# GpSimd takes three weight remainders and half of the rotated keys of an attention stage; two sums of squares move to the middle of a norm's features

## The chip, the cores and the metric

The kernel runs as one launch on one core of a Trainium2 chip. The metric is the device time of that launch in microseconds (us). The engines are named as in the profile: PE (TensorE, matrix products, PEld its weight loads), DVE (VectorE), ACT (ScalarE), POOL (GpSimd), SP (SyncE, whose queue issues the weight transfers). SBUF is the memory that all of them read; PSUM is the one that PE writes and that POOL cannot read.

## The reference

Four transformer blocks in a row work on 256 positions of width 1024, all in float32. Cut to the parts that the change touches:

```python
def mla_mixer(hn, pos, w_in, g_q_lat, w_uq, g_kv_lat, w_ukv, g_qn, g_kn, w_o):
    z = hn @ w_in
    c_q, c_kv, k_pe = z[..., :512], z[..., 512:768], z[..., 768:]
    q  = (rms_norm(c_q, g_q_lat) @ w_uq).reshape(b, s, 16, 96)
    kv = (rms_norm(c_kv, g_kv_lat) @ w_ukv).reshape(b, s, 16, 128)
    k = concatenate([kv[..., :64], broadcast(k_pe)], -1)      # 64 plain + 32 rotated parts
    q, k = rms_norm(q, g_qn), rms_norm(k, g_kn)               # per head
    q, k = rope on the last 32 parts of each
    o = block_causal_attention(q, k, kv[..., 64:])            # softmax per head, 16 heads
    return o.reshape(b, s, 1024) @ w_o
```

Around it stand SwiGLU layers (f0 to f3 in the kernel's names), gates with an embedding (p0, p1), a second attention mixer (fox) and a last block (b2), each behind an RMS norm (n0 to n8). b2 begins with norm n8: `x * rsqrt(mean(x*x) + eps)`, times a gain, then a product with a wide matrix.

## The kernel before, in words

**Weights.** All products are made from split numbers. A weight group is 128 x 2048 floats, transferred by SP into `raw`, a ring of four slots. ACT rounds it into `wh` (signal `hi_done`), DVE takes the remainder `wl = raw - wh` (signal `lo_done`), and PE multiplies three times: `wh` by the rounded activations, `wl` by them, and `wh` by their remainders (L614 to L616, L647 to L651, L926 to L934). PE waits for a group by `lo_done` (`wait_group`). SP refills a slot when `lo_done` says its remainder is made; ACT reuses a slot of `wh` when PE has set `w_used`. Each engine runs its own program in the written order, and semaphores are the only links. No scheduler moves anything.

**MLA heads.** The 16 heads run as a software pipeline over four engines. For head j: PE turns queries and keys of the head into PSUM (`turned`, L690), ACT and DVE copy them out (`copy_queries` L1682, `copy_keys` L2305), PE makes the scores (`scores`, L842 to L845), DVE reduces them to negated maxima and scales these by the inverse norm of the queries (`maxima`, L2313, L2314, and L2317 `nmx<-mxp,hrs`), ACT makes the exponentials (`exponentials`, L1692), PE turns them (`probabilities`), DVE copies them out (`copy_turned`, L2324) and takes reciprocals, PE multiplies by the values (`values`, L863), DVE writes the output (`outputs`, L2332). DVE's step i does `maxima(i-1)`, `copy_keys(i)`, `copy_turned(i-2)`, `outputs(i-3)`; PE's step i does `turned(i)`, `scores(i-1)`, `probabilities(i-2)`, `values(i-3)`. The first steps are written out in `begin`, steps from 6 on run in a loop.

The kernel begins this pipeline when only the first eight heads are ready. The second eight heads' sums, inverse norms and scalings are made inside it: DVE sums squares (`sum_keys`, `sum_queries`), POOL makes inverse norms (`inverse_rms`, L2808, L2809, where L2809 is a power) and rotates the queries (L2849 to L2852), DVE scales the keys (`scale_keys`: L2245 for the 64 plain parts, L2246 for the 32 rotated ones). `maxima(8)` waits for POOL's last inverse norm. In steps 8 to 18, DVE also makes the remainders of the weight groups g+11, g+12 and g+13 (three quarters of `mla_w_o`), a quarter of a group in a step (`split_quarter`, L1994). PE first needs group g+11 in `o_high(2)`, after the last head.

**Norm n8.** PE turns x into PSUM in pieces of 128 positions by 128 features. ACT rounds each piece, times its gain, into `zh` (`round_x`, L1505), and DVE takes the remainder `zl` (`rest_x`, L2030). `BY_FEATURES` is the order of the 16 pieces: feature block k, and within it t = 0, 1. After the 16th piece ACT makes two sums of squares (`squares`, L1493), then rounds the next weight groups of b2, which PE waits for.

Of the kernel before, what the change touches and what calls it, by code (L numbers as in the profile page):

```python
# [18 lines left out]
F32 = mybir.dt.float32  # L19
# [3 lines left out]
ALU = mybir.AluOpType  # L23
# [3 lines left out]
P = 128  # L27
S = 256
NT = S // P
# [5 lines left out]
H = 16  # L35
QR, KVR, ROPE, NOPE = 512, 256, 32, 64
DQ = NOPE + ROPE
# [5 lines left out]
RING = 4  # L43
GC = 2048
# [62 lines left out]
PLAN, NGROUPS = plan()  # L107
# [43 lines left out]
def build(nc, I, out):  # L151
    with ExitStack() as ctx:
        def sem(name):
            return ctx.enter_context(nc.semaphore(name))
# [11 lines left out]
        raw = sb("raw", [P, RING, GC])  # L166
        wh = sb("wh", [P, RING, GC], F32R)
        wl = sb("wl", [P, RING, GC], F32R)
        h = sb("h", [P, NT, D])
# [22 lines left out]
        hrs = sb("hrs", [P, 4, H])  # L192
# [30 lines left out]
        kn = x("kn", [P, NT, H * DQ])  # L223
# [10 lines left out]
        kpe = x("kpe", [P, NT, ROPE])  # L234
# [97 lines left out]
        hi_done = sem("hi_done")  # L332
        lo_done = sem("lo_done")
# [26 lines left out]
        heads_ss = sem("heads_ss")  # L360
        heads_rstd = sem("heads_rstd")
        heads_ready = sem("heads_ready")
        q_rotated = sem("q_rotated")
        max_done = sem("max_done")
        exp_done = sem("exp_done")
# [210 lines left out]
        BY_FEATURES = [(t, k) for k in range(DK) for t in range(NT)]  # L576
# [12 lines left out]
        def _(pe):  # L589
# [359 lines left out]
            g, q, f, r = PLAN["mla"]  # L949
# [53 lines left out]
            def mla_ready(i):  # L1003
                if i % 8 == 0:
                    pe.wait_ge(q_rotated, i // 8 + 1)
                    pe.wait_ge(heads_ready, NT * (i // 8 + 1))
                    fill = q + MLA_KV_FILL[i // 8] + 1
                    pe.wait_ge(acc_read[fill % 2], acc_reads(fill))

# [66 lines left out]
            g, q, f, r = PLAN["fox"]  # L1076
# [73 lines left out]
            s = (g + 2) % RING  # L1150
            for k in range(DK):
                w = slice(k * H, (k + 1) * H)
# [6 lines left out]
            for n in range(1, 6):  # L1159
                fill = q + fox_fill(n)  # L1160
                open_acc(fill)
                for k in range(2):
                    w = fox_group(n) + k
# [65 lines left out]
            g, q, f, r = PLAN["b2"]  # L1229
# [97 lines left out]
            for c in range(len(B2_CHUNKS)):  # L1327
# [6 lines left out]
                for k in range(2):  # L1334
                    w = 2 * c + k
# [103 lines left out]
        def _(act):  # L1439
# [3 lines left out]
            done = [2]  # L1443
# [47 lines left out]
            def squares(r, t):  # L1491
                rows_ready(act, r, t)
                act.activation(hn[:, t, :], h[:, t, :], ACT.Square, accum_out=ssq[:, t:t + 1])\  # L1493
                   .then_inc(sq_done, 1)
# [94 lines left out]
            g, q, f, r = PLAN["mla"]  # L1589
# [151 lines left out]
            def ple(name, nname, r, after, r_after):  # L1741

                g, q, _, _ = PLAN[name]

                def sigmoids(t):
                    for n in range(2):
                        tile_ready(act, q + n, t, g + 3)
                        act.activation(gate[:, t, 512 * n:512 * n + 512], acc(q + n, t), ACT.Sigmoid,
                                       scale=scaled(r, t)).then_inc(acc_read[(q + n) % 2], 1)

                norm(nname, r, lambda t: split_to(g + 4), True)
                for t in range(NT):
                    squares(r, t)
                sigmoids(0)
                split_to(g + 7)
                sigmoids(1)
                if after != "n8":
                    norm(after, r_after)
                    return

                for t, k in BY_FEATURES:
                    round_x(after, r_after, t, k)
                for t in range(NT):
                    squares(r_after, t)

            ple("p0", "n3", 3, "n4", 4)
            ffn("f2", 4)
# [3 lines left out]
            g, q, f, r = PLAN["fox"]  # L1771
# [38 lines left out]
            for n, c in enumerate(FOX_CHUNKS):  # L1810
                w, fill = fox_group(n), q + fox_fill(n)
# [40 lines left out]
            g, q, f, r = PLAN["b2"]  # L1852
# [112 lines left out]
        def _(dve):  # L1965
# [16 lines left out]
            def split(g, i=0):  # L1982
# [2 lines left out]
                dve.wait_ge(hi_done, g - 1 + RING * i)  # L1985
                dve.tensor_tensor(wl[:, s, 0:n], raw[:, s, 0:n], wh[:, s, 0:n].bitcast(F32), ALU.subtract)\  # L1986
                   .then_inc(lo_done, 1)

            def split_quarter(n):

                g = done[0]
                s, w = g % RING, slice(n * GC // 4, (n + 1) * GC // 4)
                dve.wait_ge(hi_done, g - 1)
                e = dve.tensor_tensor(wl[:, s, w], raw[:, s, w], wh[:, s, w].bitcast(F32), ALU.subtract)  # L1994
                if n == 3:
                    e.then_inc(lo_done, 1)
                    done[0] += 1

            def split_half(n):

# [239 lines left out]
            def scale_keys(c, t):  # L2240

                dve.wait_ge(heads_rstd, 2 * NT * c + t + 1)
                kv = heads3(kn[:, t, :], DQ)[:, 8 * c:8 * c + 8]
                by = hrs[:, 2 + t, 8 * c:8 * c + 8].unsqueeze(2)
                dve.tensor_tensor(kv[:, :, 0:NOPE], kv[:, :, 0:NOPE], by.to_broadcast([P, 8, NOPE]), ALU.mult)  # L2245
                dve.tensor_tensor(kv[:, :, NOPE:DQ], kpe[:, t, :].unsqueeze(1).to_broadcast([P, 8, ROPE]),  # L2246
                                  by.to_broadcast([P, 8, ROPE]), ALU.mult).then_inc(heads_ready, 1)


            def keys_values(c, n):  # L2250
# [124 lines left out]
            def rest_rows(done, banks):  # L2375

                for b in banks:
                    t = b // 2
                    dve.wait_ge(oh_done, done + b + 1)
                    dve.tensor_tensor(xl[:, b % 2::2, t * P:(t + 1) * P],  # L2380
                                      M[:, b, :].rearrange("p (k n) -> p k n", k=4),
                                      xh[:, b % 2::2, t * P:(t + 1) * P].bitcast(F32), ALU.subtract)\
                       .then_inc(m_read[b], 1)

            def matrix_out(g, q, r, nname):

                residual(q, g + 3, 1.0, 0)
                split_to(g + 6)
                rest(nname, r, 0)
                residual(q, g + 3, 1.0, 1)  # L2390
                split_to(done[0] + 1)
                rest(nname, r, 1)
# [3 lines left out]
            for i in range(6, H + 3):  # L2396
                if i == H + 2:
                    rest_rows(OH["mla"], range(1))
                step(i)

                if i == 6:
                    scale_keys(1, 1)
                elif i == 7:
                    sum_queries(1, 1)
                elif i >= 8:
                    split_quarter((i - 8) % 4)
                if i == H + 2:
                    split_quarter(3)
            rest_rows(OH["mla"], range(1, 4))
            matrix_out(g + 10, q + 10 + H, 2, "n2")  # L2410
            ffn("f1", 2, "n3")

# [384 lines left out]
        def _(pool):  # L2797
            steps = [0]

            def link(ins):  # L2800

                steps[0] += 1
                ins.then_inc(p_step, 1)
                pool.wait_ge(p_step, steps[0])

            def inverse_rms(dst, src, n, width, signal):

                link(pool.tensor_scalar(dst, src, 1.0 / width, EPS, ALU.mult, ALU.add))  # L2808
                pool.tensor_tensor(dst, dst, mhalf[:, 0:n], ALU.pow).then_inc(signal, 1)  # L2809
# [25 lines left out]
            for c in range(2):  # L2835
                for t in range(NT):
                    pool.wait_ge(heads_ss, 2 * NT * c + t + 1)
                    inverse_rms(hrs[:, 2 + t, 8 * c:8 * c + 8], hss[:, 2 + t, 8 * c:8 * c + 8], 8, DQ, heads_rstd)
                for t in range(NT):
                    for n in (2 * c, 2 * c + 1):  # L2840
                        fill = PLAN["mla"][1] + MLA_Q_FILL[n]
                        pool.wait_ge(acc_read[fill % 2], acc_reads(fill))
                    qv = qn[:, t, :].rearrange("p (h d) -> p h d", d=DQ)[:, 8 * c:8 * c + 8]
                    tb = [tab[:, 0, t, j, :].unsqueeze(1).to_broadcast([P, 8, 16]) for j in range(4)]
                    x1, x2 = qv[:, :, NOPE:NOPE + 16], qv[:, :, NOPE + 16:DQ]
                    pool.wait_ge(heads_sq, 2 * NT * c + NT + t + 1)
                    m4 = [rt[:, 2 * t + m // 2, 8 * (m % 2):8 * (m % 2) + 8, :] for m in range(4)]
                    for m, (x, j) in enumerate(((x1, 0), (x2, 1), (x1, 2), (x2, 3))):
                        e = pool.tensor_tensor(m4[m], x, tb[j], ALU.mult)  # L2849
                    link(e)  # L2850
                    pool.tensor_tensor(x1, m4[0], m4[1], ALU.subtract)
                    e = pool.tensor_tensor(x2, m4[2], m4[3], ALU.add)  # L2852
                    if t:
                        e.then_inc(q_rotated, 1)
                    else:
                        link(e)
                for t in range(NT):
                    pool.wait_ge(heads_ss, 2 * NT * c + NT + t + 1)
                    inverse_rms(hrs[:, t, 8 * c:8 * c + 8], hss[:, t, 8 * c:8 * c + 8], 8, DQ, heads_rstd)
            pool.wait_ge(m_ready[3], PLAN["n2"][2][3])  # L2860
            pool.wait_ge(table_out, 16)
            pool.dma_start(p_n[:, :, :], I["p"][0, 0].rearrange("(t p) n -> p t n", p=P)).then_inc(p_in, 16)
# [153 lines left out]
```

## Time and profile before

| | us |
|---|---|
| median of 3 runs | 1336.75 (1336.58 to 1338.41) |
| the profiled execution | 1337.19 |
| its span | 1335.4 |
| PE busy | 1316.5, 99% of the span |
| PEld busy | 1078.3, 81% |
| DVE busy | 798.0, 60% |
| ACT busy | 679.4, 51% |
| POOL busy | 128.8, 10% |

PE is on the chain that ended last for 88% of the span, DVE for 5%, ACT for 3%. The granted TensorE clock has a mean of 0.998 of full speed. The profiled execution lies 0.44 us above the median, and 1.8 us of it lie outside the span. The matmuls' ends overlap, so PE's pace is read from the distance of starts, not from durations. In the rows below a time at the start is us from the span's start, and what stands in brackets is the idle time of the engine just before and what ended it.

### The profile page before, as it was taken

What the parts mean: (1) busy time and instruction counts of PE and PEld (TensorE: products, weight loads), DVE (VectorE), ACT (ScalarE), POOL (GpSimd) and SP (SyncE); (2) the same over time, 40 slices, a digit from 0 to 9 for tenths busy, and PEclk for the clock granted to TensorE, in tenths of its full rate; (3) what the DMA queues carried; (4) which work ended last, traced back from release to release, by engine and by line L of the source; (5) the groups of instructions that cost most, each with busy time, mean ns of one, the idle gap of its engine ahead of it and who ended that gap; (6) DMA issues with size and microseconds to landing.
All of it is one profiled execution on the core that took longest, in us unless ns stands there. A gap on an engine that the chain in (4) does not pass through costs nothing.

```text
span 1335.4 us, 17481 instructions
## 1 busy us (share of the span) xinstructions
PE 1316.5 (99%) x6474; PEld 1078.3 (81%) x6474; DVE 798.0 (60%) x1036; ACT 679.4 (51%) x959; POOL 128.8 (10%) x199
## 2 busy tenths in 40 slices
PE   8999999999999999999999999999999999999997
PEld 6888788788888887888888777888888877788886
DVE  6755448885555546655544667655554655665674
ACT  6444427755444426644444557544443646457542
POOL 2000002712000000000000330100000042110000
PEclk9999999999999999999999999999999999999999
DMA  9665544336655654555553654466564397555441
GB/s 299 219 188 189 189 154 165 98 95 190 204 182 184 218 194 144 180 186 187 180 204 126 227 183 127 134 188 188 188 220 160 128 266 246 167 163 172 160 158 32
DMA packets 148782, 236.46 MB, mean 177 GB/s; under 512 B 10087, under 2 KB 103447, under 8 KB 148208
## 3 DMA queue, kind: packets, MB, share of 16 engines
q1 hardware_dynamic: 143600, 222.26, 51.1%
q0 software_dynamic: 4736, 12.96, 3.3%
q8 instruction: 40, 0.66, 0.2%
q10 hardware_dynamic: 384, 0.41, 0.1%
q14 instruction: 22, 0.18, 0.0%
HBM read 233.43 MB, written 4.51 MB: 178 GB/s over the span
## 4 chain that ended last, share of the span: by engine, by line
PE 88%; DVE 5%; ACT 3%; issue 2%; DMA 1%; POOL 0%; SPq 0%; POOLq 0%; DVEq 0%; ACTq 0%
PE acc L614 19%; PE acc L616 19%; PE acc L615 19%; PE acc L647 7%; PE acc L648 7%; PE acc L651 7%; PE misc L690 5%; DVE wl L1986 2%; ACT wh L1461 1%; PE misc L1270 1%; DMA raw<-in_ffn_w_in_dram 1%; PE misc L1127 1%; ACT xh L1505 0%; DVE pT L2324 0%; ACT hn L1493 0%
## 5 line engine op out<-in xcount | busy, mean ns | idle before, releaser
L1986 DVE TENSOR_TENSOR wl<-raw,wh 128x2048 fp32r<-128x2048 f32 (+2 forms) x201 | 453.2, 2261 | 266.0 <-ACT wh L1461 265.9
L1461 ACT ACTIVATE wh<-raw 128x2048 fp32r<-128x2048 f32 (+2 forms) x207 | 388.7, 1888 | 138.8 <-PE acc L651 124.7
L614 PE MATMUL acc<-wh,xh 128*128 128x512 f32 (+1 forms) x832 | 329.0, 395 | 2.8 <-DVE xl L2030 1.3
L616 PE MATMUL acc<-wh,xl 128*128 128x512 f32 (+1 forms) x832 | 323.2, 388 | 0.0
L615 PE MATMUL acc<-wl,xh 128*128 128x512 f32 (+1 forms) x832 | 322.6, 388 | 0.0
L614 PEld LDWEIGHTS acc<-wh,xh 128*128 128x128 f32 x832 | 156.3, 188 | 36.9 <-DVE wl L1979 4.4
L616 PEld LDWEIGHTS acc<-wh,xl 128*128 128x128 f32 x832 | 156.2, 188 | 32.8
L615 PEld LDWEIGHTS acc<-wl,xh 128*128 128x128 f32 x832 | 156.5, 188 | 30.1
L647 PE MATMUL acc<-wh,ah 128*128 128x512 f32 x320 | 125.7, 393 | 0.0
L648 PE MATMUL acc<-wl,ah 128*128 128x512 f32 x320 | 124.6, 389 | 0.0
L614 PE MATMUL acc<-wh,zh 128*128 128x512 f32 x272 | 108.5, 399 | 1.5 <-DVE wl L1986 1.0
L616 PE MATMUL acc<-wh,zl 128*128 128x512 f32 x272 | 106.2, 390 | 0.0
L615 PE MATMUL acc<-wl,zh 128*128 128x512 f32 x272 | 106.0, 390 | 0.0
L1550 ACT ACTIVATE ah<-misc 128x512 f32 (+1 forms) x44 | 26.4, 599 | 156.0 <-PE misc L690 156.0
L651 PE MATMUL acc<-wh,al 128*128 128x512 f32 x320 | 98.5, 389 | 0.0
L2808 POOL TENSOR_SCALAR rstd<-ssq 128x1 f32<-128x1 f32 x19 | 9.4, 493 | 924.4 <-ACT hn L1493 924.4
L1544 ACT ACTIVATE sg<-acc,rstd 128x256 f32<-128x256 f32 x88 | 41.4, 475 | 100.5 <-PE acc L616 100.5
L2146 DVE TENSOR_TENSOR al<-misc,ah 128x512 f32 (+1 forms) x44 | 30.4, 692 | 84.0 <-ACT ah L1550 84.0
L1505 ACT ACTIVATE xh<-misc,gains 128x128 fp32r<-128x128 f32 x128 | 40.4, 364 | 68.8 <-PE misc L690 59.7
L647 PEld LDWEIGHTS acc<-wh,ah 128*128 128x128 f32 x320 | 60.1, 188 | 13.8 <-issue 1.7
L651 PEld LDWEIGHTS acc<-wh,al 128*128 128x128 f32 x320 | 60.1, 188 | 12.6
L648 PEld LDWEIGHTS acc<-wl,ah 128*128 128x128 f32 x320 | 60.1, 188 | 12.2
(363 smaller groups left out, 1654.1 us busy)
## 6 DMA issues: line engine op xcount, KB each, us to landing
raw<-in_ffn_w_in_dram SPq DMA_DIRECT2D x172, 512.0 KB, 4.7
raw<-in_ffn_w_out_dram SPq DMA_DIRECT2D x88, 512.0 KB, 4.4
raw<-in_w_in_dram SPq DMA_DIRECT2D x64, 512.0 KB, 4.8
raw<-in_fox_w_in_dram SPq DMA_DIRECT2D x24, 512.0 KB, 4.4
raw<-in_ple_w_gate_dram SPq DMA_DIRECT2D x16, 512.0 KB, 4.1
raw<-in_mla_w_o_dram SPq DMA_DIRECT2D x8, 512.0 KB, 4.1
raw<-in_fox_w_o_dram SPq DMA_DIRECT2D x8, 512.0 KB, 4.5
raw<-in_w_out_dram SPq DMA_DIRECT2D x8, 512.0 KB, 4.4
```

The lines of the kernel that those rows point to most:

```text
L614: pe.matmul(dst, hi, rhs_h, start=first, stop=False)
L615: pe.matmul(dst, hi, rhs_l, start=False, stop=False)
L616: return pe.matmul(dst, lo, rhs_h, start=False, stop=last)
L647: pe.matmul(acc(q + n, t), xa, wh[:, s, r], start=st, stop=False)
L648: pe.matmul(acc(q + n, t), xa, wl[:, s, r], start=False, stop=False)
L651: mm = pe.matmul(acc(q + n, t), xb, wh[:, s, r], start=False, stop=en)
L690: return pe.transpose(M[0:rows, b, cols], src, m[:, :])
L1461: act.activation(wh[:, s, 0:n], raw[:, s, 0:n], ACT.Copy).then_inc(hi_done, 1)
L1505: act.activation(x_cols(xh, r, k, t), turned(r, k, t), ACT.Copy, scale=gains[:, c:c + 1]).then_inc(xh_done, 1)
L1544: act.activation(sg[:, c % 2, t, :], acc(q, t)[:, 0:256], ACT.Silu, scale=rstd[:, t:t + 1]).then_inc(silu_done, 1)
L1986: dve.tensor_tensor(wl[:, s, 0:n], raw[:, s, 0:n], wh[:, s, 0:n].bitcast(F32), ALU.subtract)\
L2146: dve.tensor_tensor(al[:, bass.ds(i * 4 + 2 * c, 2), :], pair(M[:, b, :]), ah[:, bass.ds(i * 4 + 2 * c, 2), :].bitcast(F32), ALU.subtract)\
```

## The change

It has three parts. (1) The remainders of weight groups g+11 to g+13 are no longer made by DVE in quarters; POOL makes them whole, one instruction of 128 x 2048 each, behind its last inverse norm of the heads. DVE waits for all three before it goes on to the output product. (2) For the second eight heads, the rotated part of the scaled keys is made by POOL, between the rotated queries and the queries' inverse norms. PE waits for it before it turns head 8. (3) In norm n8 the two sums of squares stand behind the 9th and the 10th piece instead of behind the 16th.

```diff
@@ mla_ready (PE)
                     pe.wait_ge(heads_ready, NT * (i // 8 + 1))
+                    if i:
+                        pe.wait_ge(keys_rotated, NT)
@@ ple, norm n8 (ACT)
-                for t, k in BY_FEATURES:
+                for n, (t, k) in enumerate(BY_FEATURES):
                     round_x(after, r_after, t, k)
-                for t in range(NT):
-                    squares(r_after, t)
+                    if n in (8, 9):
+                        squares(r_after, n - 8)
@@ scale_keys (DVE): the rotated part only for the first eight heads
+                if c == 0:
+                    e = dve.tensor_tensor(kv[:, :, NOPE:DQ], kpe[...], by[...], ALU.mult)
+                e.then_inc(heads_ready, 1)
@@ DVE, loop over the heads' steps
-                elif i >= 8:
-                    split_quarter((i - 8) % 4)
-                if i == H + 2:
-                    split_quarter(3)
             rest_rows(OH["mla"], range(1, 4))
+            dve.wait_ge(lo_done, g + 12)
+            done[0] = g + 14
@@ POOL, behind the rotated queries
+                if c:
+                    pool.wait_ge(heads_ready, NT)
+                    pool.wait_ge(heads_rstd, 2 * NT * c + NT)
+                    for t in range(NT):
+                        ...
+                        pool.tensor_tensor(kv[:, :, NOPE:DQ], kpe[...], by[...], ALU.mult)\
+                            .then_inc(keys_rotated, 1)
                 for t in range(NT):
                     pool.wait_ge(heads_ss, 2 * NT * c + NT + t + 1)
                     inverse_rms(...)
@@ POOL, behind the heads
+            g = PLAN["mla"][0]
+            for n in range(g + 11, g + 14):
+                pool.wait_ge(hi_done, n - 1)
+                pool.wait_ge(lo_done, n - 2)
+                pool.tensor_tensor(wl[:, n % RING, :], raw[:, n % RING, :], wh[:, n % RING, :].bitcast(F32),
+                                   ALU.subtract).then_inc(lo_done, 1)
```

DVE, one step of the heads' loop and the start of the next, before (L1994 is the quarter of a remainder, L2317 the scaled maxima):

```order
L2313 TENSOR_REDUCE mxp<-acc 128x1
L2314 TENSOR_REDUCE mxp<-acc 128x1
L2317 TENSOR_TENSOR nmx<-mxp,hrs 128x2
L2305 TENSOR_SCALAR qkT<-misc,headg 96x256
L2324 COPY pT<-misc 128x384
L2326 RECIPROCAL rin<-rs 128x2
L2332 TENSOR_TENSOR hn<-misc,rin 128x2x64
L1994 TENSOR_TENSOR wl<-raw,wh 128x512
L2313 TENSOR_REDUCE mxp<-acc 128x1
```

The same place now, where the scaled maxima are L2314:

```order
L2310 TENSOR_REDUCE mxp<-acc 128x1
L2311 TENSOR_REDUCE mxp<-acc 128x1
L2314 TENSOR_TENSOR nmx<-mxp,hrs 128x2
L2302 TENSOR_SCALAR qkT<-misc,headg 96x256
L2321 COPY pT<-misc 128x384
L2323 RECIPROCAL rin<-rs 128x2
L2329 TENSOR_TENSOR hn<-misc,rin 128x2x64
L2310 TENSOR_REDUCE mxp<-acc 128x1
```

The quarter behind `outputs` is gone from the step, and the rest keeps its order.

POOL, from the second eight heads' last rotated queries to the transfers behind the heads, before:

```order
L2849 TENSOR_TENSOR rt<-qn,tab 128x128 x4
L2851 TENSOR_TENSOR qn<-rt 128x8x16
L2852 TENSOR_TENSOR qn<-rt 128x8x16
L2808 TENSOR_SCALAR hrs<-hss 128x8
L2809 TENSOR_TENSOR hrs<-hrs,mhalf 128x8
L2808 TENSOR_SCALAR hrs<-hss 128x8
L2809 TENSOR_TENSOR hrs<-hrs,mhalf 128x8
L2862 DMA p_n<-in_p_dram 128x2x256
```

The same place of POOL now, with the keys (L2860) and the remainders (L2870):

```order
L2845 TENSOR_TENSOR rt<-qn,tab 128x128 x4
L2847 TENSOR_TENSOR qn<-rt 128x8x16
L2848 TENSOR_TENSOR qn<-rt 128x8x16
L2860 TENSOR_TENSOR kn<-kpe,hrs 128x8x32 x2
L2804 TENSOR_SCALAR hrs<-hss 128x8
L2805 TENSOR_TENSOR hrs<-hrs,mhalf 128x8
L2804 TENSOR_SCALAR hrs<-hss 128x8
L2805 TENSOR_TENSOR hrs<-hrs,mhalf 128x8
L2870 TENSOR_TENSOR wl<-raw,wh 128x2048 x3
L2874 DMA p_n<-in_p_dram 128x2x256
```

The two key instructions stand ahead of both inverse norms of the queries, the three long remainders behind them.

ACT at norm n8, now (before, the 16 `zh` stand in one row of x16 with both sums of squares behind it):

```order
L1751 ACTIVATE gate<-acc,rstd 128x512 x2
L1508 ACTIVATE zh<-misc,gains 128x4x32 x9
L1496 ACTIVATE hn,ssq<-h 128x1024
L1508 ACTIVATE zh<-misc,gains 128x4x32
L1496 ACTIVATE hn,ssq<-h 128x1024
L1508 ACTIVATE zh<-misc,gains 128x4x32 x6
L1464 ACTIVATE wh<-raw 128x2048 x4
```

Both sums of squares now stand ahead of the last six pieces, and the weight groups follow the 16th piece directly.

## Rows read from the trace of the kernel before

**Rows 1.** Busy time in a stretch: PE, PEld, DVE, ACT, POOL, clock, DMA.

```profile
272.00:280.00 8.00, 7.85 (x64) 6.63 (x62) 7.81 (x27) 6.01 (x18) 0.00 (x0) 1.00 0.00 1
```

**Rows 2.** Chain that ended last, in the heads' loop: start, us, what.

```profile
276.52 0.60 DVE wl L1994
277.32 0.34 DVE mxp L2314
```

**Rows 3.** Timeline of DVE in the heads: scaled maxima of heads 8, 10, 11, 15; a quarter.

```profile
272.58 0.16 DVE L2317 TENSOR_TENSOR nmx<-mxp,hrs 128x2 f32<-128x2 f32 x1
...
277.69 0.16 DVE L2317 TENSOR_TENSOR nmx<-mxp,hrs 128x2 f32<-128x2 f32 x1
...
278.92 0.68 DVE L1994 TENSOR_TENSOR wl<-raw,wh 128x512 fp32r<-128x512 f32 x1
...
280.17 0.16 DVE L2317 TENSOR_TENSOR nmx<-mxp,hrs 128x2 f32<-128x2 f32 x1
...
290.09 0.17 DVE L2317 TENSOR_TENSOR nmx<-mxp,hrs 128x2 f32<-128x2 f32 x1
```

**Rows 4.** Timeline of PE in the heads' loop: scores, turned heads, scores again.

```profile
255.28 0.39 PE L842 MATMUL acc<-qkT 96*128 96x128 f32 x2
...
275.85 0.49 PE L842 MATMUL acc<-qkT 96*128 96x128 f32 x2
...
277.73 0.38 PE L690 MATMUL misc<-ident,qn 128*96 128x128 f32 x2
277.95 0.38 PE L690 MATMUL misc<-ident,kn 128*96 128x128 f32 x2
278.33 0.49 PE L842 MATMUL acc<-qkT 96*128 96x128 f32 x2
```

**Rows 5.** Timeline of DVE, the second eight heads' rotated keys.

```profile
263.30 0.67 DVE L2246 TENSOR_TENSOR kn<-kpe,hrs 128x256 f32<-128x256 f32 x1
...
266.38 0.41 DVE L2246 TENSOR_TENSOR kn<-kpe,hrs 128x256 f32<-128x256 f32 x1
```

**Rows 6.** Timeline of POOL in and ahead of the heads.

```profile
230.59 0.20 POOL L2808 TENSOR_SCALAR hrs<-hss 128x8 f32<-128x8 f32 x1 [8.22 <-DVE hss L2232]
...
246.28 3.56 POOL L2809 TENSOR_TENSOR hrs<-hrs,mhalf 128x8 f32<-128x8 f32 x1
...
252.21 1.64 POOL L2809 TENSOR_TENSOR hrs<-hrs,mhalf 128x8 f32<-128x8 f32 x1
...
260.58 0.46 POOL L2849 TENSOR_TENSOR rt<-qn,tab 128x128 f32<-128x128 f32 x1
...
261.00 0.88 POOL L2849 TENSOR_TENSOR rt<-qn,tab 128x128 f32<-128x128 f32 x2
...
269.90 1.65 POOL L2809 TENSOR_TENSOR hrs<-hrs,mhalf 128x8 f32<-128x8 f32 x1
```

**Rows 7.** Timeline of DVE, instructions that lie beside those of POOL.

```profile
246.04 2.29 DVE L1986 TENSOR_TENSOR wl<-raw,wh 128x2048 fp32r<-128x2048 f32 x1
...
253.58 0.16 DVE L2317 TENSOR_TENSOR nmx<-mxp,hrs 128x2 f32<-128x2 f32 x1
...
260.68 0.38 DVE L2317 TENSOR_TENSOR nmx<-mxp,hrs 128x2 f32<-128x2 f32 x1
```

**Rows 8.** Chain that ended last, behind norm n8.

```profile
1069.42 2.18 ACT hn L1493 x4
1071.60 1.82 ACT wh L1461
1073.44 2.30 DVE wl L1986
```

**Rows 9.** Timeline of PE and of ACT around norm n8.

```profile
1075.88 0.47 PE L614 MATMUL acc<-wh,zh 128*128 128x512 f32 x1 [0.96 <-DVE wl L1986]
...
1067.32 0.62 ACT L1505 ACTIVATE zh<-misc,gains 128x128 fp32r<-128x128 f32 x2 [1.23 <-DVE zl L2030]
```

**Rows 10.** Busy time and granted clock (third last number) behind PE's last product.

```profile
1328.00:1330.00 2.00, 0.00 (x0) 0.00 (x0) 0.42 (x1) 0.72 (x2) 0.56 (x2) 0.91 0.00 0
```

More of the change, by code:

```diff
@@ L362, in build @@
         heads_ready = sem("heads_ready")
+        keys_rotated = sem("keys_rotated")
         q_rotated = sem("q_rotated")
@@ L1987, in split @@
                    .then_inc(lo_done, 1)
[L1989 to L1997, printed above, removed]
             def split_half(n):
@@ L2244, in scale_keys @@
                 by = hrs[:, 2 + t, 8 * c:8 * c + 8].unsqueeze(2)
-                dve.tensor_tensor(kv[:, :, 0:NOPE], kv[:, :, 0:NOPE], by.to_broadcast([P, 8, NOPE]), ALU.mult)
-                dve.tensor_tensor(kv[:, :, NOPE:DQ], kpe[:, t, :].unsqueeze(1).to_broadcast([P, 8, ROPE]),
-                                  by.to_broadcast([P, 8, ROPE]), ALU.mult).then_inc(heads_ready, 1)
+                e = dve.tensor_tensor(kv[:, :, 0:NOPE], kv[:, :, 0:NOPE], by.to_broadcast([P, 8, NOPE]), ALU.mult)
+                if c == 0:
+                    e = dve.tensor_tensor(kv[:, :, NOPE:DQ], kpe[:, t, :].unsqueeze(1).to_broadcast([P, 8, ROPE]),
+                                          by.to_broadcast([P, 8, ROPE]), ALU.mult)
+                e.then_inc(heads_ready, 1)
             def keys_values(c, n):
@@ L2856, in _ @@
                         link(e)
+                if c:
+                    pool.wait_ge(heads_ready, NT)
+                    pool.wait_ge(heads_rstd, 2 * NT * c + NT)
+                    for t in range(NT):
+                        kv = kn[:, t, :].rearrange("p (h d) -> p h d", d=DQ)[:, 8 * c:8 * c + 8]
+                        by = hrs[:, 2 + t, 8 * c:8 * c + 8].unsqueeze(2)
+                        pool.tensor_tensor(kv[:, :, NOPE:DQ], kpe[:, t, :].unsqueeze(1).to_broadcast([P, 8, ROPE]),
+                                           by.to_broadcast([P, 8, ROPE]), ALU.mult).then_inc(keys_rotated, 1)
                 for t in range(NT):
```

## The prediction

> **What bounds the kernel now.** I first read the busy times: PE is busy for 99% of the span, so only time in which PE waits, or a stage whose pace another engine sets, can be gained. The list of waits by engine then shows where PE waits at all. Two places matter here.
>
> The first is the heads' loop. In [rows 1] PE and DVE both look full, 7.85 and 7.81 of 8 us, so busy shares do not tell which one leads. The chain does: in the loop it runs through DVE's quarter of a remainder and DVE's maxima [rows 2]. One head takes 280.17 - 277.69 = 2.48 us on DVE [rows 3], and DVE never rests. PE has a small gap: its scores start at 275.85, its last pair of turned tiles at 277.95, and such a pair takes 0.22 (277.73 to 277.95), so PE could go on at 278.17 but does at 278.33 [rows 4]. PE's own work is 2.32 us a head. Where PE did not have to wait, the first two score products are 0.10 shorter (0.39 against 0.49) [rows 4], so its floor is 2.22 to 2.32; I take 2.27.
>
> The second is the beginning of the last block. PE stands still for 0.96 us there for a weight remainder [rows 9]. The chain behind it is ACT's sums of squares, 2.18 us, then ACT's rounding, then DVE's remainder [rows 8].
>
> **Part 1, the three remainders.** Removed from DVE: twelve quarters, 0.60 us of the path each (0.68 with its overlap) [rows 2, 3], eight of them between the maxima of heads 7 and 15. DVE's step falls from 2.48 to 1.88, below PE's 2.27, so PE becomes the bound of a free-running loop. The gain there is 2.48 - 2.27 = 0.21 a head.
>
> Added on POOL: three subtractions of 128 x 2048. No row has one. POOL's nearest is the product of 128 x 128 in two SBUF inputs, whose starts lie 0.42 apart (260.58, 261.00) [rows 6]. The fixed part of a POOL instruction is at most the 0.20 of its shortest scaling [rows 6], which leaves 0.22 for 128 elements, and 0.20 + 16 x 0.22 = 3.7 us for 2048. With no fixed part it is 16 x 0.42 = 6.7 us. A fixed part of 0.15 gives 4.5 us; I take this, near the low end, because some of the 0.20 is the scaling's own work but a fixed part there must be. Three of them are 13.5 us. POOL is free for them: its last inverse norm ends at 269.90 + 1.65 = 271.55 [rows 6], and PE wants the first of the three groups only after head 15's maxima at 290.09 [rows 3]. By time alone POOL's work is hidden, with some 5 us to spare, and the slots of `raw` come free no later than now. The wait that DVE gets behind the heads is then met long before. The Trainium skill has 4497 ns for this very size (GPSIMD Engine Reference, "Elementwise — side-by-side cycle accounting"); no run here shows it yet, and by it the sum would be the same.
>
> What is not hidden is the memory path that POOL and DVE share. Two rows show it. POOL's power of 128 x 8 takes 1.64 us alone, but 3.56 when it is issued 0.24 after DVE has begun a subtraction with two SBUF inputs that runs from 246.04 to 248.33 [rows 6, 7]: POOL stood for the whole rest of DVE's instruction. The other way round, DVE's `nmx`, with two SBUF inputs of two elements each, is 0.16 long everywhere in the loop, but 0.38 at 260.68, where it ends at 261.06, just when POOL's product of 260.58 gives way to the next at 261.00 [rows 6, 7]. Two elements need no bandwidth; DVE waited until that POOL instruction was through, and was let in before the following one. So I read: a DVE instruction with two SBUF inputs waits for the end of a POOL instruction that is reading SBUF. Against it stands one row: `nmx` at 253.58 is not delayed inside POOL's power of 252.21 to 253.85 [rows 6, 7]. That power reads only 8 elements and computes for the rest, so its reading was over; a subtraction of 2048 elements reads to its end.
>
> The Trainium skill states it as a rule that speaks against this change (SBUF — State Buffer, "Who interferes with whom"): a DVE instruction with two SBUF inputs and a GpSimd instruction that reads SBUF exclude each other for a whole instruction, whichever came first. By that rule, the rows for 128 elements agree; for 2048 no run here shows it.
>
> In DVE's step `nmx` is that instruction, and everything is queued behind it: ACT's exponentials of the head wait for it, and `copy_keys` of the next head, for which PE's next scores wait. Now the sum. The queries' last inverse norm ends about 271.3 (0.3 earlier, part 2). The first subtraction begins there; `nmx` of head 8, before at 272.58, wants to run at about 272 and waits until 271.3 + 4.5 = 275.8. Once it is through (about 0.15 for the handover), the second subtraction begins. `nmx` of head 9 comes 2.3 us later (keys, scores, maxima), inside it, and waits until 280.4. Head 10 waits likewise until 285.1, and ends at about 285.3. Before it ended at 277.85 [rows 3]: 7.4 later. From head 10 to 15 five heads run at 2.27 instead of 2.48, which gives back 1.05. Part 1 with its price: +6.4 us. With subtractions of 3.7 it is +4.0, with 5.3 +8.8, with 6.7 +13.
>
> **Part 2, the rotated keys.** DVE loses 0.67 + 0.41 busy [rows 5], of which 0.60 and 0.33 lie on its path. POOL gets two products of 128 x 256, by the same rate 0.7 us each (0.64 to 0.84), behind the rotated queries. The first of them lies just where `nmx` of head 5 now comes and holds it back by about 0.6, so I count 0.3 gained, not 0.9. POOL is done with them more than 1 us before PE turns head 8, so the new wait costs nothing; were it not so, PE would lose a few tenths. POOL's first inverse norm of the queries comes 1.4 later and has 4 us of rest behind it to absorb that. The 0.3 is in the start of 271.3 above and otherwise vanishes in the stall of head 8. Bounds for the part alone: 0 to 0.9 gained.
>
> **Part 3, the squares.** ACT rests 1.23 us before 1067.32 and about as long before the piece ahead of it [rows 9]; both rests were for DVE or PE. One sum of squares is 2.18 / 2 = 1.09 us of the path. Both fit in the rests, and the last six pieces come about 0.1 later. PE has several products in hand for each piece and does not wait in this stretch, so a tenth is hidden. ACT's rounding for the group that PE waits for begins about 2 us sooner, so the 0.96 of PE's waiting [rows 9] goes. What is late next is nothing: PE follows with the small products for the row norms, whose inverse norms also come sooner. Gain 0.9, bounds 0 (if a transfer sets the group) and 0.96. POOL's transfers behind n8 start 2 to 3 us sooner and meet the weight loads; PE has several us in hand there.
>
> **Sum.** +6.4 - 0.9 = +5.5 on the profiled execution's 1337.19: 1342.7; on the median 1336.75: 1342.2 us. Its own range, from subtractions of 3.7 to 5.3 us and part 3 between 0 and 0.96, is 1339.8 to 1345.6.
>
> **The rivals.**
>
> *Rival 1, `nmx` slips through (faster).* If POOL's reads leave room for a two-element read, no head is held. Then `nmx` of head 8 runs at 272.0 instead of 272.58, seven heads to head 15 run at 2.27 instead of 17.51 / 7 = 2.50 [rows 3], together -2.2; with part 3, -3.1: 1333.7 us. For it: `nmx` at 253.58. Against it: the 0.22 at 260.68 for two elements, and POOL's 1.9 us of standing at 246.28.
>
> *Rival 2, the stall also costs clock or is longer (slower still).* PE rests 2 to 3.4 us at a time in the three stalls. At the end of the kernel PE has no work from 1328.00 on, and the granted clock has a mean of 0.91 over 1328 to 1330 [rows 10]: it falls from full (2.4 GHz) to half (1.2 GHz) at about 1329.6. If that happens in the heads, some PE steps behind the stalls run at half speed: 2 to 4 us more, 1345 to 1346. If POOL starts its next subtraction before DVE is let in, head 8 waits for all three: 271.3 + 13.5 = 284.8 instead of 272.6, less the gains: +12.2 - 1.5 - 0.9, 1346.6. Against it: DVE was let in at 261.00.
>
> *Rival 3, the lock is held in pieces (no change).* If DVE waits about 1 us each time, three or six such waits eat the gains: about 1336.5 us. Only a POOL instruction that pauses in its reading would do so; no row shows one.
>
> **How the numbers follow.** A difference of 0.2%, 2.7 us, is about what a measurement of this kernel can tell from none. Forecast 0.68, rival 1 0.20, rival 2 0.07, rival 3 0.05. Faster by over 0.2%: rival 1 with most of its weight (its 3.1 us are just over the bound) and nothing else, 0.17. Within: the rest of rival 1, rival 3, a small part of the forecast, 0.12. Slower: 0.71. The time is the forecast's, 1342.2. The range has to take in rival 1 to leave out no more than 2 in 10: 1333.3 to 1346.5.
>
> **What would show it.** In the profile of the changed kernel: `nmx` instructions of 2 to 4 us for heads 8, 9 and 10, each ending with a POOL subtraction of about 4.5 us; PE's scores 4.6 us apart there and 2.3 apart from head 11 on; the last `nmx` at about 296.5 instead of 290.09; no PE wait of 0.96 at the third group of the last block. If `nmx` stays at 0.16 beside a subtraction, my reading of the shared path is wrong and rival 1 holds. If the subtractions are far from 4.5 us, the size is wrong threefold.

## The result and the profile after

| | us | against before |
|---|---|---|
| before, median of 4 runs | 1336.74 | |
| after, median of 4 runs (1342.9 to 1346.11) | 1343.8 | 1.0052 [1.004, 1.0065] |
| the profiled execution of after | 1342.9 | before 1337.19 |
| its span | 1341.1 | before 1335.4 |

The change makes the kernel slower by 7.1 us; 1342.2 was predicted. The two profiled executions differ by 5.7 us: the profiled execution of after is the fastest of its four.

First the stretch of [rows 1] in the changed kernel: length, then PE, PEld, DVE, ACT, POOL busy, granted clock, DMA share, GB/s.

```profile
272.00:280.00 8.00, 3.41 (x20) 2.81 (x20) 7.51 (x10) 2.94 (x9) 7.71 (x3) 0.79 0.41 131
```

PE worked 7.85 of these 8 us before, in 64 instructions, and 3.41 now, in 20. DVE's 7.51 are in 10 instructions instead of 27: it is "busy" because it stands inside one of them. The timeline of DVE shows which; these are the scaled maxima of heads 5, 8, 9, 10, 11, 12, 13 and 15, and answer to [rows 3]:

```profile
263.27 0.34 DVE L2314 TENSOR_TENSOR nmx<-mxp,hrs 128x2 f32<-128x2 f32 x1
...
271.24 3.51 DVE L2314 TENSOR_TENSOR nmx<-mxp,hrs 128x2 f32<-128x2 f32 x1
...
276.98 2.43 DVE L2314 TENSOR_TENSOR nmx<-mxp,hrs 128x2 f32<-128x2 f32 x1
...
282.53 1.55 DVE L2314 TENSOR_TENSOR nmx<-mxp,hrs 128x2 f32<-128x2 f32 x1
...
287.18 0.16 DVE L2314 TENSOR_TENSOR nmx<-mxp,hrs 128x2 f32<-128x2 f32 x1
...
289.67 0.17 DVE L2314 TENSOR_TENSOR nmx<-mxp,hrs 128x2 f32<-128x2 f32 x1
...
292.10 0.16 DVE L2314 TENSOR_TENSOR nmx<-mxp,hrs 128x2 f32<-128x2 f32 x1
...
296.96 0.16 DVE L2314 TENSOR_TENSOR nmx<-mxp,hrs 128x2 f32<-128x2 f32 x1
```

The timeline of POOL for the same time (the keys' rotated part, its last inverse norm, the remainders):

```profile
262.99 1.18 POOL L2860 TENSOR_TENSOR kn<-kpe,hrs 128x256 f32<-128x256 f32 x2
...
268.62 1.64 POOL L2805 TENSOR_TENSOR hrs<-hrs,mhalf 128x8 f32<-128x8 f32 x1
270.22 13.83 POOL L2870 TENSOR_TENSOR wl<-raw,wh 128x2048 fp32r<-128x2048 f32 x3
```

The wide view gives the three subtractions in one row; narrower windows give the second and third apart:

```profile
274.88 4.52 POOL L2870 TENSOR_TENSOR wl<-raw,wh 128x2048 fp32r<-128x2048 f32 x1
...
279.54 4.51 POOL L2870 TENSOR_TENSOR wl<-raw,wh 128x2048 fp32r<-128x2048 f32 x1
```

Add the durations. The maxima of heads 8, 9 and 10 end at 271.24 + 3.51 = 274.75, 276.98 + 2.43 = 279.41 and 282.53 + 1.55 = 284.08. The subtractions end at 270.22 + 4.51 = 274.73, 279.40 and 284.05. Three instructions that need 0.16 us each end within 0.03 us of a GpSimd instruction's end, and DVE is let in before GpSimd's next one begins (274.88, 279.54).

PE stands behind them. Its scores in the timeline, to be read against [rows 4]:

```profile
275.20 0.49 PE L843 MATMUL acc<-qkT 96*128 96x128 f32 x2 [3.26 <-DVE qkT L2302]
...
284.52 0.80 PE L843 MATMUL acc<-qkT 96*128 96x128 f32 x2
...
287.99 0.39 PE L843 MATMUL acc<-qkT 96*128 96x128 f32 x2
...
290.32 0.49 PE L843 MATMUL acc<-qkT 96*128 96x128 f32 x2
...
292.75 0.49 PE L843 MATMUL acc<-qkT 96*128 96x128 f32 x2
```

The wait is put down to `qkT`, DVE's copy of the keys, which stands behind `nmx` in DVE's order. The same two products take 0.80 at 284.52 and 0.49 later: the clock had fallen. Two-microsecond windows of the same columns show when:

```profile
276.00:278.00 2.00, 2.00 (x15) 1.91 (x13) 1.64 (x3) 1.19 (x2) 2.00 (x1) 0.67 0.88 254
...
284.00:286.00 2.00, 1.98 (x8) 1.30 (x7) 1.19 (x5) 1.45 (x5) 0.05 (x1) 0.50 0.35 80
286.00:288.00 2.00, 2.00 (x16) 1.82 (x15) 1.44 (x5) 0.62 (x3) 0.00 (x0) 0.77 1.05 351
288.00:290.00 2.00, 2.00 (x20) 1.84 (x19) 1.45 (x7) 0.96 (x4) 0.00 (x0) 1.00 0.36 128
```

A mean of 0.67 over 276 to 278 puts the fall from full to half level (2.4 to 1.2 GHz) at 276.7, after PE had done nothing from 271.9 to 275.2. The 0.77 puts the return at 286.9.

In the last block, the place of [rows 9] has no wait any more: PE goes from its small products for the norm to the next group's.

```profile
1080.49 1.08 PE L1352 MATMUL misc<-ident,rstd 128*1 128x64 f32 x8
1081.50 0.50 PE L615 MATMUL acc<-wh,zh 128*128 128x512 f32 x1
```

**Where the time went.** I take the distance from `nmx` of head 4 (start 260.68 before, 260.01 after) to `nmx` of head 15 (290.09 [rows 3], 296.96): 29.41 before, 36.95 after, +7.54 us. The last block gives back 0.96. The changed run also reached the heads 0.67 earlier. Of this, 0.64 is there already in the kernel's first 28 us (PE starts the same product at 27.72 before and at 27.08 after), far ahead of anything that was changed; in the ten experiments that product starts anywhere between 26.99 and 27.67. So this part is chance. 7.54 - 0.96 - 0.67 = 5.9, against 5.7 of difference in span.

### The profile page after: what moved, and what is told of

It reads as the page before. It is cut to its first block, busy times and chain, and to the rows that moved or that the text cites. A ratio compares the mean times of both kernels' runs of the same rounds, so it can differ in the third digit from the quotient of the medians.

```text
span 1341.1 us, 17477 instructions
## 1 busy us (share of the span) xinstructions
PE 1320.5 (98%) x6474; PEld 1082.0 (81%) x6474; DVE 797.5 (59%) x1022; ACT 679.1 (51%) x959; POOL 145.0 (11%) x204
## 3 DMA queue, kind: packets, MB, share of 16 engines
HBM read 233.43 MB, written 4.51 MB: 177 GB/s over the span
## 4 chain that ended last, share of the span: by engine, by line
PE 90%; DVE 4%; ACT 3%; issue 2%; DMA 0%; POOL 0%; SPq 0%; POOLq 0%; DVEq 0%; ACTq 0%
PE acc L615 20%; PE acc L617 19%; PE acc L616 19%; PE acc L648 7%; PE acc L649 7%; PE acc L652 7%; PE misc L691 5%; DVE wl L1990 1%; ACT wh L1464 1%; PE misc L1273 1%; PE misc L1130 1%; PE acc L845 1%; DMA raw<-in_ffn_w_in_dram 0%; ACT xh L1508 0%; PE misc L864 0%
```

## The experiments

**The theories.** Their letters are those of the expectations below. A is the forecast's: a DVE instruction with two SBUF inputs waits for the whole of a GpSimd instruction that reads SBUF, and all of the loss is behind that. Its rivals: B, the loss comes from something else in the change (the keys on POOL, the squares). C, every DVE instruction that reads SBUF waits for a GpSimd subtraction. And one without a letter: the loss comes from bandwidth or transfers, in which case it would depend neither on the form of `nmx` nor on the length of POOL's instructions. What was open besides is why the pace behind the stalls was not what I had forecast. Theory D is about that: scores, maxima, keys and the next scores follow one another, and this ring sets the pace once DVE has no quarters to make. All ratios below are against the kernel before, run on the same chip beside the experiment; a ratio is known to about 0.1%, some 1.2 us.

**1. Part 1 undone.** The rest of the change (keys on POOL, squares moved) stays.

```diff
+                elif i >= 8:
+                    split_quarter((i - 8) % 4)
+                if i == H + 2:
+                    split_quarter(3)
...
-            dve.wait_ge(lo_done, g + 12)
-            done[0] = g + 14
...
-                pool.tensor_tensor(wl[:, n % RING, :], raw[:, n % RING, :], wh[:, n % RING, :].bitcast(F32),
-                                   ALU.subtract).then_inc(lo_done, 1)
```

> The changed kernel with part 1 undone: the twelve quarters are back on VectorE, the rotated keys stay on GpSimd, the squares stay in the middle. Theory A (GpSimd's long subtractions hold VectorE's nmx): no nmx over 0.5 us from head 8 on, clock at full in the heads, heads as before less 0 to 0.9 us, last block 0.9 us shorter: 1335.4 to 1336.0 us. Theory B (the rotated keys or the moved squares are what costs): 1340 us or more.

Measured: 1335.65 us, 0.9991 [0.9982, 1.0]. `nmx` is 0.16 to 0.17 from head 8 to 15. The heads are 2.48 apart but for two (2.63 from head 8 to 9, 2.85 from head 10 to 11). The whole loss is part 1, which excludes B.

**2. Part 1 alone on the kernel before.**

```diff
-                elif i >= 8:
-                    split_quarter((i - 8) % 4)
-                if i == H + 2:
-                    split_quarter(3)
...
+            dve.wait_ge(lo_done, g + 12)
+            done[0] = g + 14
...
+                pool.tensor_tensor(wl[:, n % RING, :], raw[:, n % RING, :], wh[:, n % RING, :].bitcast(F32),
+                                   ALU.subtract).then_inc(lo_done, 1)
```

> The kernel before with part 1 alone. Theory A: three nmx of 2.4 to 3.5 us, each ending with a subtraction of 4.6 us, clock at half level behind the second stall, 7.0 to 8.0 us over the kernel before: 1344 to 1345 us. Theory B (the keys on GpSimd or the squares cost): about 1336 us.

Measured: 1346.06 us, 1.0069 [1.0056, 1.0083], 9.3 us over before, where I had expected 7.0 to 8.0. `nmx` of heads 8 to 10 takes 3.51, 2.23 and 1.55, nearly as in after. What differs is the clock, here in windows from 286 and from 290:

```profile
286.00:288.00 2.00, 2.00 (x10) 1.63 (x9) 0.65 (x3) 0.41 (x2) 0.00 (x0) 0.50 0.87 232
...
290.00:292.00 2.00, 2.00 (x17) 1.79 (x17) 0.84 (x4) 0.49 (x2) 0.00 (x0) 0.89 0.00 0
```

It stays at half until about 290.4, 3.5 us longer than in after:

```profile
288.02 0.16 DVE L2317 TENSOR_TENSOR nmx<-mxp,hrs 128x2 f32<-128x2 f32 x1
...
291.79 0.16 DVE L2317 TENSOR_TENSOR nmx<-mxp,hrs 128x2 f32<-128x2 f32 x1
```

From head 11 to 12 it takes 3.77 instead of 2.49 in after: 1.3 us that the same three stalls cost more.

**3. Part 3 alone on the kernel before.**

```diff
+                for n, (t, k) in enumerate(BY_FEATURES):
                     round_x(after, r_after, t, k)
-                for t in range(NT):
-                    squares(r_after, t)
+
+                    if n in (8, 9):
+                        squares(r_after, n - 8)
```

> The kernel before with part 3 alone. Theory A: the PE wait of 0.96 us at the third weight group of the last block is gone and nothing replaces it: 0.9 to 1.0 us under the kernel before, 1335.8 us. Rival: the gain is given back by a later wait for a transfer, 1336.7 us.

Measured: 1335.79 us, 0.9991 [0.9982, 1.0]. The heads are as before (29.40 from head 4 to 15) and PE's longest wait for a remainder at L614 falls from 0.96 to 0.3. That is 1.0 us for part 3, and it leaves 0.14 for part 2, the difference of the medians to experiment 1, which is too small to tell from nothing.

**4. Another form of `nmx`.** One edit on after: two instructions that take the factor as a scalar for each partition, so that none has two SBUF tensors as inputs.

```diff
-                    dve.tensor_tensor(nmx[:, :, j], mx, hrs[:, 0:NT, j], ALU.mult).then_inc(max_done, 1)
+                    for t in range(NT):
+                        e = dve.tensor_scalar(nmx[:, t, j:j + 1], mx[:, t:t + 1], hrs[:, t, j:j + 1], None, ALU.mult)
+                    e.then_inc(max_done, 1)
```

> The changed kernel, but nmx made by two instructions with one SBUF tensor and a pointer scalar each, so that no VectorE instruction in the loop has two SBUF tensors. Theory A (only the second SBUF tensor input collides with GpSimd's reads): no stall, the three subtractions run beside the heads, clock stays full; the added instruction costs 0.1 us a head; about 1336 us, 7 to 8 under the changed kernel. Theory C (any VectorE instruction that reads SBUF waits for a GpSimd subtraction): the stalls of 2.4 to 3.5 us stay, 1343 to 1345 us.

Measured: 1336.05 us, 0.9992 [0.9983, 1.0001]. DVE's maxima of heads 9 to 11, and POOL beside them:

```profile
274.55 0.33 DVE L2315 TENSOR_SCALAR nmx<-mxp,hrs 128x1 f32<-128x1 f32 x2
...
277.11 0.33 DVE L2315 TENSOR_SCALAR nmx<-mxp,hrs 128x1 f32<-128x1 f32 x2
...
279.67 0.33 DVE L2315 TENSOR_SCALAR nmx<-mxp,hrs 128x1 f32<-128x1 f32 x2
```

```profile
270.73 13.88 POOL L2872 TENSOR_TENSOR wl<-raw,wh 128x2048 fp32r<-128x2048 f32 x3
```

The subtractions, the slots and the transfers are those of after, and every stall is gone. This excludes bandwidth and transfers. It excludes C too, since the new instructions read SBUF as well. But the heads are 2.56 apart although DVE has no quarter to make: freeing DVE did not speed up the loop. Some of the 2.56 is the new form, which takes 0.33 for the two instructions instead of 0.16.

**5. The same work in short instructions.** After with each remainder in eight pieces of 256, `nmx` as it was.

```diff
+                for c in range(0, GC, 256):
+                    e = pool.tensor_tensor(wl[:, n % RING, c:c + 256], raw[:, n % RING, c:c + 256],
+                                           wh[:, n % RING, c:c + 256].bitcast(F32), ALU.subtract)
+                e.then_inc(lo_done, 1)
```

> The changed kernel with each GpSimd remainder cut into eight instructions of 128 x 256; nmx is the one with two SBUF tensors again. Theory A (the wait lasts to the end of the GpSimd instruction that is running, and VectorE gets in before the next): each piece takes 0.7 us, 24 of them 16.5 us, nmx is 0.2 to 0.85 long beside them and never more, clock stays full, 1336 to 1338 us. Rival (VectorE waits until GpSimd's whole row of instructions is through): one nmx of 15 us, 1349 us.

Measured: 1336.31 us, 0.9995 [0.9986, 1.0004]. DVE, then POOL:

```profile
273.85 0.51 DVE L2314 TENSOR_TENSOR nmx<-mxp,hrs 128x2 f32<-128x2 f32 x1
...
276.59 0.69 DVE L2314 TENSOR_TENSOR nmx<-mxp,hrs 128x2 f32<-128x2 f32 x1
...
287.90 0.17 DVE L2314 TENSOR_TENSOR nmx<-mxp,hrs 128x2 f32<-128x2 f32 x1
```

```profile
270.18 16.84 POOL L2871 TENSOR_TENSOR wl<-raw,wh 128x256 fp32r<-128x256 f32 x24
```

Now `nmx` waits at most 0.69 - 0.16 = 0.53 us, which is less than one piece (16.84 / 24 = 0.70), and not at all once the pieces are through at 287.02. Same engine, same bytes: what counts is the length of the instruction that holds the path. With experiment 4 this shows A.

**6, 7, 8. DVE copies the keys ahead of the maxima.** If `nmx` only hurt because the keys' copy stands behind it, and if the loop is slow because scores, maxima, keys and the next scores lie in a row, the other order in DVE's step should help. Tried on experiments 4, 5 and 3:

```diff
                 def step(i):
-                    if 0 <= i - 1 < H:
-                        maxima(i - 1)
                     if i < H:
                         copy_keys(i)
+                    if 0 <= i - 1 < H:
+                        maxima(i - 1)
```

> The kernel with the pointer-scaled nmx (e4), and in VectorE's step the keys of head i are copied ahead of the maxima of head i-1. Theory D (without VectorE's quarters one head takes 2.56 us because scores, maxima, keys and the next scores follow one another in series): the pace falls to PE's own 2.2 to 2.35 us a head, nine heads gain 1.9 to 2.5 us, about 1334.0 us. Rival (another bound of VectorE, ScalarE or PE): the pace stays at 2.45 to 2.56, 1336 us.

> The pieces of 128 x 256 (e5) with the keys copied ahead of the maxima. Theory D with A: nmx still waits up to 0.85 us now and then, but off the series that sets the pace, so 2.2 to 2.4 us a head and 1334 to 1335 us. Rival: the waits still show, 1336 us or more.

> The kernel before with the squares moved (e3) and the keys copied ahead of the maxima, the quarters still on VectorE. Theory D: VectorE's own 2.48 us a head is the bound there, so the new order gains nothing to speak of: 1335.8 us, within 0.4 of e3. Rival (the order alone is what counts, wherever the remainders are made): 1334 us.

Measured: 1343.7 us, 1.0051 [1.0038, 1.0065]; 1343.06, 1.0044 [1.0031, 1.0058]; 1341.95, 1.0035 [1.0023, 1.0047]. All three missed by 6 to 10 us. The chain that ended last in experiment 6 tells why:

```profile
267.06 0.37 ACT qkT L1685
...
267.55 0.48 DVE qkT L2302
268.03 0.20 DVE mxp L2310
268.23 0.34 DVE mxp L2311
...
268.72 0.21 DVE nmx L2315
...
269.32 0.74 ACT probs L1695 x3
270.06 0.94 ACT wh L1472
271.00 0.37 ACT qkT L1685
...
271.50 0.48 DVE qkT L2302
```

The keys' copy waits until ACT has copied the queries of the same head, and those stand in ACT's order behind the exponentials of the head two before, which wait for its `nmx`. Put behind the keys, `nmx` closes a longer ring over two engines: 3.95 us a head while ACT also makes halves of weight groups, about 3.0 after. I had looked at DVE's order alone and overlooked ACT's. The clock has a share in two of the three: by its means in windows of two us it is at half level from 275.2 to 285.4 in experiment 6 and from 273.8 to 280.6 in experiment 7, but at full level throughout the heads in experiment 8. So the 6.2 us of experiment 8 over experiment 3 are the order alone; how much of the rest in the other two is the clock is not worked out. A version that drops the keys' wait for the queries was not tried.

**9, 10. The keys of heads 10 to 15 on ACT.** This takes the 0.48 of the keys' copy off the ring scores, maxima, keys, scores, without any change in what waits for what on DVE. Experiment 9 has it on experiment 4, experiment 10 on experiment 1 (part 1 undone).

```diff
+                    if 10 <= i < H:
+                        tb = i % 2
+                        act.activation(qkT[0:DQ, tb, S:2 * S], M[0:DQ, tb, S:2 * S], ACT.Copy,
+                                       scale=headg[0:DQ, 1:2]).then_inc(m_read[tb], 1)
...
-                    if i < H:
+                    if i < 10:
                         copy_keys(i)
```

> The kernel with the pointer-scaled nmx and GpSimd's remainders (e4), and from head 10 on ScalarE copies the keys as well as the queries, so that VectorE's maxima no longer stand between a head's scores and the next head's keys. Theory D (the pace of 2.56 us a head is a series of scores, maxima, keys, scores; the order tried in e6 failed because the keys waited for ScalarE's queries behind the exponentials): with the keys behind the queries on ScalarE the pace falls to PE's own 2.2 to 2.35 us from head 10 on, 1.3 to 2.0 us under e4, 1334.0 to 1334.8 us. Rival (ScalarE's exponentials and two copies become the series): 2.5 us a head or more, 1336 us.

> The same on the kernel with VectorE's quarters (e1): VectorE's step falls from 2.48 to 2.08 us, below PE's. Theory D: 2.2 to 2.35 us a head from head 10 on, 0.8 to 1.6 us under e1, 1334.1 to 1334.9 us, so the remainders need not leave VectorE at all. Rival (as above): 1335.7 us or more.

Measured: 1334.06 us, 0.9976 [0.9966, 0.9986], as expected, and 1333.38 us, 0.997 [0.9959, 0.9982], 0.7 below what I expected. Both are faster than before and after. PE's scores of heads 10 to 12 in experiment 10:

```profile
274.53 0.40 PE L843 MATMUL acc<-qkT 96*128 96x128 f32 x2
...
276.86 0.39 PE L843 MATMUL acc<-qkT 96*128 96x128 f32 x2
...
279.07 0.39 PE L843 MATMUL acc<-qkT 96*128 96x128 f32 x2
```

They are 2.33 and 2.21 apart, and PE runs on: this is the floor of 2.22 to 2.32 that the forecast took from [rows 4]. DVE makes its quarters in this kernel and reaches the floor all the same; with the quarters gone (experiment 9) it is no faster. For theory D the clean comparison is experiment 9 with 4, where DVE was not full in either: 2.56 a head became 2.31 to 2.33. In experiment 10 the keys' copy also leaves a DVE that was full, so that a lighter DVE could have brought the gain there.

The distance from `nmx` of head 4 to head 15, less 1.0 us for part 3, accounts for every kernel within 0.6 us:

| | heads 4 to 15 | difference to before, with part 3 | measured (medians) |
|---|---|---|---|
| before | 29.41 | | |
| after | 36.95 | +6.5 | +7.1 |
| experiment 1 | 29.15 | -1.3 | -1.2 |
| 2 (no part 3) | 38.84 | +9.4 | +9.3 |
| 4 | 29.21 | -1.2 | -0.8 |
| 5 | 30.34 | -0.1 | -0.4 |
| 6 | 36.81 | +6.4 | +7.0 |
| 7 | 36.75 | +6.3 | +6.3 |
| 8 | 35.58 | +5.2 | +5.2 |
| 9 | 27.38 | -3.0 | -2.7 |
| 10 | 27.14 | -3.3 | -3.4 |

## Why the prediction was right, and what in it was wrong

**The mechanism of part 1 was right.** It was read from 0.22 us in one row, `nmx` at 260.68 [rows 7], and 1.9 us in another, POOL's power at 246.28 [rows 6], and experiments 4 and 5 show it. The Trainium skill's rule (SBUF — State Buffer, "Who interferes with whom") is borne out for an instruction of 2048 elements, with 3.51, 2.43 and 1.55 us. It is not borne out for POOL's power. The row that stood against the forecast, `nmx` of 0.16 us inside the power of 252.21 [rows 6, 7], comes again in the changed kernel: `nmx` of head 7 starts at 268.81 and takes 0.17, inside the power of 268.62 to 270.26. That a power is done reading early, as the forecast has it, no run tests.

**The size of a subtraction was right:** 4.5 predicted, 4.51 measured. In part this was a choice: the rows of before bound it only between 3.7 and 6.7, and the fixed part of 0.15 us that makes it 4.5 stands in none of them. With 3.7 or 5.3 the forecast would have been 2.4 us off its own number. The Trainium skill's 4497 ns (GPSIMD Engine Reference, "Elementwise — side-by-side cycle accounting") agrees within 0.02 us.

**Place of the stalls: right within 1.2 us.** I put the first subtraction at 271.3 and the end of `nmx` of head 10 at 285.3; they are 270.22 and 284.08. DVE's steps ahead of head 8 came sooner, 0.67 by chance and as much again by part 2. From `nmx` of head 4 (start) to the end of that of head 10 it is 17.17 us before (260.68 to 277.85) and 24.07 after: +6.9, where the sum had +7.4.

**The failed step is the term behind the stalls.** The prediction says "From head 10 to 15 five heads run at 2.27 instead of 2.48, which gives back 1.05." It counted DVE's and PE's busy time of a step and left out the ring of waits between them, and it put the clock at nothing. From the end of `nmx` of head 10 to the start of that of head 15 it was 12.24 before and is 12.88 after: 0.64 lost, not 1.05 gained. Two things are in it.
- The pace. Free of the quarter, the heads are 2.43 apart (289.67, 292.10), which gives back 0.25. I had compared DVE's busy 1.88 with PE's 2.27 and taken the larger. The loop is neither: DVE waits for PE's scores in each step.

```profile
289.78 0.48 DVE L2302 TENSOR_SCALAR qkT<-misc,headg 96x256 f32<-96x256 f32 x1
...
291.45 0.29 DVE L2310 TENSOR_REDUCE mxp<-acc 128x1 f32<-128x128 f32 x1 [0.46 <-PE acc L846]
```

  Scores, maxima, `nmx`, keys and the next scores follow one another: the keys' copy ends at 290.26, PE's scores run from 290.32 to 291.41, the maxima from 291.45, `nmx` at 292.10, and PE's next scores start at 292.75, 2.43 after the last. The quarter had filled a hole in this ring. Its removal brings 0.05 a head; in experiment 4 the longer `nmx`, which lies in the ring, makes it 2.56. Experiment 9 shows that taking the keys' copy out of the ring brings 0.24 a head.
- The clock, which I had made a rival with 0.07. From the end of `nmx` of head 10 to the start of the next it is 3.10 us (284.08 to 287.18); at full clock it is 2.27 (289.83 to 292.10), and so it was behind the first stall, before the clock fell: 2.23 (274.75 to 276.98), against 3.12 behind the second (279.41 to 282.53). With 2.49 instead of 2.43 for the next head (287.18 to 289.67) that is 0.9 lost. -0.25 + 0.9 = +0.65, the measured 0.64.

**Part 2: right in the total.** The two products with the keys take 1.18 together, below the 0.64 to 0.84 each of the forecast, and `nmx` of head 5 is held for 0.34 - 0.16 = 0.18, not for 0.6. So the heads from 4 to 8 take 11.26 in experiment 1 and 11.89 in experiment 3: 0.63 gained by head 8, not 0.3. But 0.37 of it is gone again at head 11, the 2.85 of experiment 1, for a reason that is open, and 0.25 is left at head 15. The new wait of PE costs nothing.

**Part 3: right.** 0.9 predicted, 0.96 in the trace and 1.0 in experiment 3.

**The sum.** Parts 1 and 2 came to +7.5 in place of +6.4, part 3 to -1.0 in place of -0.9. That the profiled execution (1342.9) lies only 0.2 from the 1342.7 predicted for it is luck: the time behind the stalls was 1.69 above the forecast's, but the stalls came 0.5 under the sum and the start 0.67 early by chance. The median of 1343.8 is 1.6 above the forecast, inside its own range of 1339.8 to 1345.6. The three executions of after without a trace took 0.5 to 3.2 us longer, at a mean granted clock of 0.993 against 0.995 in the profiled one. The 0.9 us of clock are therefore the price in the fastest execution; what it was in the others is not shown.

**The rivals.** Rival 1 (`nmx` slips through) fell with the first stall. Its time of 1333.7 would not have come even so: experiment 4 has no stall and takes 1336.05, since a loop free of quarters does not run at 2.27. (Its longer `nmx` is in that time: at 2.43 a head instead of 2.56 it would be 0.9 less by my estimate, still 1.4 above 1333.7.) Rival 2's half about the clock happened, with 0.9 us where I had 2 to 4; in experiment 2 it was 0.9 + 1.3 = 2.2. PE stood still for 3.26 and 1.40 us in the first two stalls and not at all in the third, where its own work at half clock filled the time. The half about POOL did not happen: its next subtraction always began after DVE's `nmx`. Rival 3 did not happen in the change, but experiment 5 is that case made on purpose; it came to 1336.31, where I had given 1336.5.

**What stays open:** why the half clock lasted 3.5 us longer in experiment 2 than in after, with stalls of nearly the same length and place; and what held head 11 back by 0.37 us in experiment 1.

## What to carry to other kernels

Idle time of GpSimd was not free here, because its instructions shared something with one on the path. Before moving work to GpSimd, look at every DVE instruction with two SBUF inputs that will run beside it, however small, at what is queued behind it, and at the length of each single GpSimd instruction. If the work must go there, give the small DVE instruction its factor as a per-partition scalar, or cut GpSimd's work into short pieces; the first took every stall away here, the second left at most 0.53 us of each. And when two engines both look full, walk the ring of waits over all engines before counting a removed instruction as a gain: the quarter removed from DVE brought 0.05 us a head, and the key copy moved from DVE to ACT brought about 2 us (experiment 9 against 4, and 10 against 1, each by its difference to before).

## What the runs showed of the hardware that I had not expected

- A DVE instruction of 0.16 us on two elements a partition was held for up to 3.35 us by one GpSimd instruction. DVE is let in between two GpSimd instructions even where these stand back to back: `nmx` ends at 274.75, between the end of the first at 274.73 and the start of the second at 274.88.
- GpSimd is not slowed by it: three subtractions take 13.83 us beside the held DVE and 13.88 beside one that is never held. In eight pieces each they take 16.84.
- DVE's multiplication by a per-partition scalar, 128x1, ran beside the subtractions in 0.21 us, two of them in 0.33, with no wait in heads 8 to 12, which lie beside them.
- The clock's fall at 276.7 came 1.5 us after PE had ended its pause of 3.3 us, and it came back at 286.9, although PE is busy for 5.98 of the 6 us from 280 to 286. In experiments 6 and 7 it fell too, though PE's longest wait in the heads is 0.9 and 1.3 us there. Nearly the same stalls cost 0.9 us more by the clock in the changed kernel and 2.2 in experiment 2.
